# The last expert of a streamed mixture of experts leaves its loop: a new block order, an activations buffer of its own, two result banks, and slot numbers read ahead

## The reference

```python
def expert_choice_ffn(h, w_router, w1, w3, w2):
    cap = EC_CAPACITY * L // N_EXPERTS
    aff = jax.nn.softmax((h @ w_router).astype(jnp.float32), axis=-1)
    gate, idx = lax.top_k(aff.transpose(0, 2, 1), cap)
    xs = jax.vmap(lambda hb, ib: hb[ib])(h, idx)
    a = jnp.einsum('becd,edf->becf', xs, w1)
    b = jnp.einsum('becd,edf->becf', xs, w3)
    y = jnp.einsum('becf,efd->becd', jax.nn.silu(a) * b, w2) * gate[..., None].astype(h.dtype)
    return jax.vmap(lambda yb, ib: jnp.zeros((L, D), yb.dtype).at[ib.reshape(-1)].add(yb.reshape(-1, D)))(y, idx)
```

## Time and profile before

| | |
|---|---|
| median of 3 runs | 2743.27 us (2742.66 to 2746.19) |
| the profiled execution's own time | 2747.89 us |
| its span in the trace | 2746.1 us |
| PE busy | 2543.1 us (93%) |
| chain that ended last | 63% PE, 22% DMA, 11% DVE |

### The profile page before, as it was taken

The page is one execution under the profiler, slowest core; times in us unless marked ns, Lnnn a source line. Parts: engine busy times, 40 slices in busy tenths (PEclk is TensorE's granted clock), DMA queues, the critical chain, the costliest instruction groups (busy, mean ns, idle before and its releaser), DMA issues.

```text
span 2746.1 us, 80150 instructions
## 1 busy us (share of the span) xinstructions
PE 2543.1 (93%) x31510; PEld 1936.7 (71%) x31510; DVE 1166.4 (42%) x2033; ACT 818.5 (30%) x3460; POOL 980.0 (36%) x2992
## 2 busy tenths in 40 slices
PE   6998999999997899999789999999999959999995
PEld 3555676666745899888746566776666559998984
DVE  3997534665425011111268874356653331111114
ACT  3112223443213443333021132334331233333320
POOL 2373233232201255445435633133221014454453
PEclk9999999999998999999989999999999979999998
DMA  8332311212236899999633322211132249999993
GB/s 328 120 131 92 110 57 53 75 53 105 80 122 267 345 427 428 428 427 427 274 130 123 130 92 90 75 49 64 61 138 83 105 178 396 428 427 428 428 428 134
DMA packets 43854, 572.39 MB, mean 208 GB/s; under 512 B 5248, under 2 KB 5376, under 8 KB 8320
## 3 DMA queue, kind: packets, MB, share of 16 engines
q1 hardware_dynamic: 40032, 550.52, 49.5%
q10 hardware_dynamic: 2592, 16.38, 1.5%
q0 software_dynamic: 1024, 3.15, 0.4%
HBM read 561.11 MB, written 8.91 MB: 208 GB/s over the span
## 4 chain that ended last, share of the span: by engine, by line
PE 63%; DMA 22%; DVE 11%; issue 2%; ACT 1%; DVEq 0%; POOL 0%; ACTq 0%; POOLq 0%; SPq 0%
PE ps L462 47%; DMA ring<-in_w_exp 12%; PE ps L629 6%; DMA region_b<-in_w_exp 6%; DVE region_b L1659 5%; DMA region_x<-in_w_exp 4%; PE ps L884 3%; PE ps L850 1%; PE ps L833 1%; PE ps L821 1%; PE ps L996 1%; DVE region_r L1948 0%; DVE rstd L1573 0%; DVE region_r L1947 0%; ACT region_r L2274 0%
## 5 line engine op out<-in xcount | busy, mean ns | idle before, releaser
L2266 POOL TENSOR_TENSOR region_m<-region_m,region_r 128x8 f32 x2416 | 433.2, 221 | 559.6 <-DVE region_r L1987 504.9
L462 PE MATMUL ps<-region_r,ring 128*64 128x80 f32 x12096 | 445.8, 234 | 30.4 <-DMA ring<-in_w_exp 17.2
L462 PEld LDWEIGHTS ps<-region_r,ring 128*64 128x64 f32 x12096 | 434.2, 138 | 40.3 <-issue 22.5
L462 PE MATMUL ps<-hT,ring 128*128 128x320 f32 (+2 forms) x1440 | 431.6, 442 | 8.2 <-ACT hT L1169 8.2
L2274 ACT ACTIVATE region_r<-hT 128x8 f32 x2410 | 292.0, 204 | 281.7 <-DVE region_r L1999 153.3
L462 PEld LDWEIGHTS ps<-hT,ring 128*128 128x128 f32 x1440 | 257.7, 192 | 146.9 <-issue 68.3
L462 PE MATMUL ps<-region_r,region_b 128*64 128x80 f32 x8064 | 298.2, 235 | 42.3 <-DMA region_b<-in_w_exp 20.7
L462 PEld LDWEIGHTS ps<-region_r,region_b 128*64 128x64 f32 x8064 | 290.6, 138 | 49.3 <-DVE region_r L2276 18.7
L1659 DVE SCALAR_TENSOR_TENSOR region_b<-region_b,params 128x655 f32<-128x655 f32 x240 | 278.0, 1158 | 8.5
L462 PE MATMUL ps<-region_b,ring 128*128 128x320 f32 x560 | 182.5, 435 | 0.0
L462 PE MATMUL ps<-region_r,region_x 128*64 128x80 f32 x4032 | 152.3, 237 | 16.0 <-DMA region_x<-in_w_exp 8.3
(11 more groups left out here) (281 smaller groups left out, 3425.6 us busy)
## 6 DMA issues: line engine op xcount, KB each, us to landing
ring<-in_w_exp SPq DMA_DIRECT2D x90, 2048.0 KB, 24.7
region_b<-in_w_exp SPq DMA_DIRECT2D x60, 2048.0 KB, 24.6
ring<-in_w_mix SPq DMA_DIRECT2D x39, 2048.0 KB, 8.1
region_x<-in_w_exp SPq DMA_DIRECT2D x30, 2048.0 KB, 24.7
ring<-in_w_pair SPq DMA_DIRECT2D x32, 1536.0 KB, 6.3
region_b<-in_w_first SPq DMA_DIRECT2D x4, 2048.0 KB, 13.8
ring<-in_w_ada SPq DMA_DIRECT2D x4, 2048.0 KB, 10.0
ring<-in_w_first SPq DMA_DIRECT2D x3, 2048.0 KB, 11.6
```

Of the source, the lines that this page charges most:

```text
L462: ins = pe.matmul(*args, **kw)
L2266: last = eng.tensor_tensor(x[:, :, token], x[:, :, token], y_gated[e % 2][:, :, c:c + 1], ALU.add)
```

## The change

There are four parts, all in the expert stage of both layers.

1. PE's loop ends one turn earlier (experts 1 to 14). The last eight blocks are written out behind it, in another order: a, b, a, b of expert 15, then both downs of expert 14, then both of expert 15. `LAST_ORDER` makes SP fetch the blocks in that order. The order of slots is as before.
2. Expert 15 writes its activations to `act_last`, so they needn't wait until the downs of expert 14 have read `act`.
3. Down results go to two banks in turn, and a down block waits only for the copy of the second last one (`y_copied` starts at 2).
4. DVE loads the slot numbers of its share of experts 14 and 15 ahead of the copies that precede the adds, and POOL those of expert 15 ahead of its wait for `y_scaled`. The shares move: POOL takes 44 and 34 slots (before: 48 and 40), DVE 36 and 46 (before: 32 and 40).

```diff
-HELPED = 48
+HELPED = (44, 34)
+LAST_ORDER = (91, 92, 90, 93)
...
-        act = region_r[:, 4608:4608 + KC * CAP].rearrange("p (f c) -> p f c", f=KC)
+        act, act_last = [region_r[:, at:at + KC * CAP].rearrange("p (f c) -> p f c", f=KC) for at in (4608, 5248)]
+        y_banks = [PS[1][:, 0, 0:HC], PS[2][:, 0, 0:HC]]
...
                 def expert_block(n):
+                    if 0 <= n - LAST_ORDER[2] < len(LAST_ORDER):
+                        n = LAST_ORDER[n - LAST_ORDER[2]]
...
-                def down_block(i, n, turns):
+                def down_block(i, half, n, turns, moving=act):
 
                     need("y_copied", i - 1)
                     need("act_ready", i - 1)
-                    expert_block(n, turns, y_ps, act, "y_done")
+                    expert_block(n, turns, y_banks[half], moving, "y_done")
...
-                with pe.Fori(1, NE) as e:
+                with pe.Fori(1, NE - 1) as e:
                     need("xs_ready", e)
                     up_blocks(2 * e, FIRST_BLOCKS, e - 1, False)
-                    down_block(2 * e, FIRST_BLOCKS + 2, e - 1)
+                    down_block(2 * e, 0, FIRST_BLOCKS + 2, e - 1)
                     up_blocks(2 * e + 1, FIRST_BLOCKS + 3, e - 1, False)
-                    down_block(2 * e + 1, FIRST_BLOCKS + 5, e - 1)
-                for b in range(LAST_BLOCKS):
-                    need("y_copied", HALVES - 1 + b)
-                    need("act_ready", HALVES)
-                    expert_block(FIRST_BLOCKS + LOOP_BLOCKS + b, 0, y_ps, act, "y_done")
+                    down_block(2 * e + 1, 1, FIRST_BLOCKS + 5, e - 1)
+                at = EXP_BLOCKS * NE - 8
+                need("xs_ready", NE - 1)
+                up_blocks(HALVES - 2, at, 0, False)
+                up_blocks(HALVES - 1, at + 2, 0, False)
+                for b in range(4):
+                    down_block(HALVES - 2 + b, b % 2, at + 4 + b, 0, act if b < 2 else act_last)
...
-                    need("y_copied", j + 2)
+                    need("y_copied", j + 3)
...
-                v.sem_inc(S["y_copied"], 1)
+                v.sem_inc(S["y_copied"], 2)
...
-                    if e:
+                    if 0 < e < NE - 1:
                         copy_y(i - 2)
...
+                helped = list(slot_columns(nc, mybir.EngineType.DVE, index, NE - 2, HELPED[0], CAP))
+                copy_y(HALVES - 4)
+                copy_y(HALVES - 3)
                 need("y_scaled", HALVES - 2)
                 need("y_added", NE - 2)
-                add_slots(nc, v, mybir.EngineType.DVE, index, NE - 2, x, y_gated, HELPED, CAP).then_inc(S["y_helped"], 1)
+                add_slots(v, helped, NE - 2, x, y_gated).then_inc(S["y_helped"], 1)
+                helped = list(slot_columns(nc, mybir.EngineType.DVE, index, NE - 1, HELPED[1], CAP))
                 copy_y(HALVES - 2)
                 copy_y(HALVES - 1)
...
-                add_slots(nc, v, mybir.EngineType.DVE, index, NE - 1, x, y_gated, CAP // 2, CAP).then_inc(S["x_ready"], 1)
+                add_slots(v, helped, NE - 1, x, y_gated).then_inc(S["x_ready"], 1)
...
+                    last = e == NE - 1
+                    count = HELPED[e - NE + 2] if e >= NE - 2 else CAP
+                    columns = slot_columns(nc, mybir.EngineType.Pool, index, e, 0, count)
+                    columns = list(columns) if last else columns
                     need("y_scaled", 2 * e + 2)
...
-def add_slots(nc, eng, which, index, e, x, y_gated, c0, c1):
-
-    for c, token in slot_columns(nc, which, index, e, c0, c1):
+def add_slots(eng, columns, e, x, y_gated):
+
+    for c, token in columns:
         last = eng.tensor_tensor(x[:, :, token], x[:, :, token], y_gated[e % 2][:, :, c:c + 1], ALU.add)
     return last
```

More of the change, by code:

```diff
@@ L177 @@
     xs_first=3, xs_parked=15, xs_ready=15, a_done=32, b_done=32, b_used=32, sil_ready=32, act_ready=32,
-    gates_wide=3, gates_in=3, index_ready=9, y_done=32, y_copied=33, y_scaled=32, y_added=15, y_helped=1, x_ready=2, sq_act=5, sq_dve=3, sq_pool=1, sq_sum=1)
+    gates_wide=3, gates_in=3, index_ready=9, y_done=32, y_copied=34, y_scaled=32, y_added=15, y_helped=1, x_ready=2, sq_act=5, sq_dve=3, sq_pool=1, sq_sum=1)
 def _layout(parts):
@@ L1073, in layer @@
                 a_ps, b_ps = PS[0][:, 0, 0:HC], PS[0][:, 1, 0:HC]
-                y_ps = PS[1][:, 0, 0:HC]
                 def spread_gates():
@@ L1983, in copy_y @@
                     gates = gates_wide[:, e, :]
-                    v.tensor_tensor(y_gated[e % 2][:, rows, :], PS[1][:, 0, 0:HC].rearrange("p (k c) -> p k c", k=4),
+                    v.tensor_tensor(y_gated[e % 2][:, rows, :], y_banks[half].rearrange("p (k c) -> p k c", k=4),
                                     gates.unsqueeze(1).broadcast_to([P, 4, CAP]), ALU.mult).then_inc(S["y_copied"], 1)
-                    need("y_copied", j + 2)
+                    need("y_copied", j + 3)
                     v.tensor_tensor(y_gated[e % 2][:, rows, :], y_gated[e % 2][:, rows, :], token_gates[:, rows, :],
                                     ALU.mult).then_inc(S["y_scaled"], 1)
-                v.sem_inc(S["y_copied"], 1)
+                v.sem_inc(S["y_copied"], 2)
                 for i in range(HALVES):
@@ L1999, in layer @@
                         v.tensor_copy(flat(xs), flat(xs_next)).then_inc(S["xs_ready"], 1)
-                    if e:
+                    if 0 < e < NE - 1:
                         copy_y(i - 2)
                     if half:
-                        link(v.tensor_tensor(flat(act)[:, HC:2 * HC], PS[0][:, 1, 0:HC], sil[1], ALU.mult), "b_used")
-                        v.tensor_copy(flat(act)[:, 0:HC], sil[0]).then_inc(S["act_ready"], 2)
+                        into = flat(act if e < NE - 1 else act_last)
+                        link(v.tensor_tensor(into[:, HC:2 * HC], PS[0][:, 1, 0:HC], sil[1], ALU.mult), "b_used")
+                        v.tensor_copy(into[:, 0:HC], sil[0]).then_inc(S["act_ready"], 2)
                     if i == HALVES - 2 and l + 1 < LAYERS:
@@ L2234, in add_rows @@
                         need("y_added", e)
-                    last = e == NE - 1
                     if last:
                         need("y_helped", 1)
-                    slots_here = {NE - 1: CAP // 2, NE - 2: HELPED}.get(e, CAP)
-                    ins = add_slots(nc, g, mybir.EngineType.Pool, index, e, x, y_gated, 0, slots_here)
-                    ins.then_inc(S["x_ready" if last else "y_added"], 1)
+                    add_slots(g, columns, e, x, y_gated).then_inc(S["x_ready" if last else "y_added"], 1)
                 for e in range(NE):
```

## The result

| | before | changed |
|---|---|---|
| median | 2745.68 us (9 runs, 2742.66 to 2749.48) | 2754.27 us (9 runs, 2752.46 to 2761.03) |
| ratio of changed to before | | 1.0034, 95% interval 1.0025 to 1.0042 |
| profiled execution, span | 2747.89, 2746.1 us | 2754.27, 2752.5 us |

The change makes the kernel slower by about 9 us. The forecast was 2739.5 us with a range up to 2746.0.

The account below looks back on a forecast made before the run. The weight stream bounds the loop, so only stage ends change. Shorter tails gain 8.3 us; late code costs 1.6 and 2.9 us, leaving 3.8 us: from the median of 2743.27 to 2739.5 us, range 2733.0 to 2746.0.

Parts of the forecast that it names:

- six loads x 0.605 = 3.7: DVE behind block 93: its six loads of slot numbers for expert 15 take 0.605 us each, 3.7 us together.
- DVE's line of the sum: DVE's copies, adds, loads and waits behind block 93 end 17.1 us after it, 2 us before POOL.
- that sign: In the changed profile, POOL and not DVE would release the squares at the end of the stage.
- that sum: POOL's chain from block 93's end to the squares takes 19.1 us; 8.3 us gained over both layers.
- Code loads: PE's straight code behind the loop arrives late at blocks 89 to 92: block 93 1.6 and 2.9 us late.
- mostly hidden: Rival: PE's code loads cost nothing or little, so block 93 doesn't move; gain 8.3 us, 2735.0 us; chance 0.36.
- PE's two waits: Blocks 94 and 95: waits for expert 15's activations and the bank's copy, 4.15 us in layer 1, would go.
- The slower rival: PE's code loads wait longer behind the full weight queue; beyond a 7.65 us period, over 5.5 us slower; chance 0.13.
- code load period: Time between PE's restarts on newly loaded code, one block each: forecast 6.1 us, no gain from 6.7 us on.
- The bound at POOL: Behind block 93, POOL's adds and loads end last, 19.1 us after it; DVE ends 2 us earlier.

Follow-up runs that it names:

- The two experiments that restore the loads' starts: The changed kernel with DVE's share of expert 15 from slot 36 (ratio 0.9981), and with its shares kept but slot-number loads cut at multiples of eight (0.9982).
- other cuts: The changed kernel with its shares kept (34 and 46) but slot-number loads cut at multiples of eight: 2741.93 us, ratio 0.9982 to the kernel before.
- the order alone: The changed kernel without its early loads and new shares, keeping the block order, expert 15's own buffer and two banks: 2746.42 us, ratio 1.0002 to the kernel before.

## Why the prediction was wrong

- **The step that failed** is the term "six loads x 0.605 = 3.7" in DVE's line of the sum. It measured 11.1 us. That made DVE's line about 24.5 us long and not 17.1, so DVE's copies held POOL up, and the tail was 25.1 and 25.2 us and not 19.1. POOL released the squares, as I had forecast, but 6 us a layer later and only because it waited for DVE; that sign came true for another reason. The two experiments that restore the loads' starts gave 18.7 to 18.9 us, so the rest of that sum was right to 0.4 us. With the shares of the change and aligned cuts the ratio was 0.9982, about 5 us of gain (2.5 to 7.4 by the interval), where I had forecast 3.8. The 12 us between the forecast (a gain of 3.8) and the traces (a loss of 8.2) all lie in this tail.
- **Why I missed it.** I took the price of a load from the window 2700 to 2724, where all started at multiples of eight, and changed their starts without asking. The row over the whole execution of the kernel before gave a warning that I passed by:

```profile
L2256 POOLq TENSOR_LOAD <-region_r x320: 561/573/1180, 855.6 to 2720.5; - x160
L2256 DVEq TENSOR_LOAD <-region_r x20: 604/606/1646, 875.3 to 2721.0; - x20
```

  The longest belong to the gathers of expert 0, where DVE's share starts at slot 69 and POOL's at 75: six numbers in 1.65 us (1.41 in layer 1), five in 1.18, against eight in 0.6.
- **Code loads**: right in kind. I forecast that block 93 ends 1.6 us late in layer 1 and 2.9 in layer 0; it was 2.1 and 2.3. That the sums agree (4.5 and 4.4 us) is partly luck: the runs with shares 44 and 36, with other cuts and with the order alone have the same code on PE, and in them block 93 was 1.6 to 3.4 us late, 4.4 to 6.4 for both layers. The restarts were 6.2, 6.3 and 5.4 us apart in layer 1 and 6.6, 5.5 and 4.9 in layer 0, forecast 6.1 (5.3 for the last in layer 0). That they are "mostly hidden" (Trainium skill, Runtime: NRT & Kernel Launch, "Instruction fetch mechanics") doesn't hold here while weights stream: the last turn written out alone costs 0.17%. Once the stream had ended (blocks 93 to 95) there was no stall, and there the page and the trace agree.
- **PE's two waits**: they went, as forecast; PE ended 8.9 us after block 93 and not 13.4 to 13.7, and its clock stayed at 1.00 in both tails.
- **The slower rival** had the sign right and the mechanism wrong. It rested on a code load period beyond 6.7 us. The true price was in the loads of registers. For POOL's I had allowed 1 us a layer more, and for DVE's only that they might be cheaper than I took.
- **The bound at POOL** was right once the loads were mended: in the run with a share from 36, POOL released the squares 2.2 us after DVE had ended, where I had forecast 2.

## What to carry to other kernels

A price read from a trace holds for the form it was read from. When a change moves a start or a size, look at the longest and shortest of that instruction over the whole execution, not at the window where it will stand. Two slots that DVE took from POOL (34 and not 36) saved 0.3 us of POOL's adds a layer (6.07 us against 6.34), and the tail was 6.2 to 6.5 us a layer longer with them.

To write out the last turn of a loop makes new code. Here the turn ran while the DMA engines were full, and its code arrived late. An order that suits every turn kept the code in the loop, and the stalls were gone.

## What the hardware showed that I had not expected

- A TENSOR_LOAD of eight numbers took 0.60 to 0.62 us when its first number lay on a multiple of four slots (16 bytes) and 1.84 to 1.96 us otherwise, on DVE; four took 0.35 and 0.96 to 0.99 us, two 0.52 to 0.55 us from any start that I tried (16 to 21). On POOL five numbers from slot 75 took 1.18 us, and eight from multiples of eight 0.57. The Trainium skill (Runtime: NRT & Kernel Launch, "Instruction fetch mechanics") gives about 200 ns a register, for loads that the runtime puts in. The slow form here, with 0.23, comes near it, and the fast one with 0.075 doesn't. Why the start matters, no run here shows.
- Straight code of PE, 16 KB a block, let PE run on every 5.4 to 6.6 us while the engines streamed weights, where PE needs 4.6 us for a block.
